# Winograd-Strassen products of an MLP: three products added from PSUM to two accumulators each, the square on ScalarE, all weight remainders on VectorE

## The reference

```python
for l in range(DEPTH):                                   # DEPTH = 2
    ...                                                  # two attention groups, output projection
    u = _rmsnorm(h, g_mlp[l])
    h = h + jnp.square(jax.nn.relu(u @ w_up[l])) @ w_down[l]   # 1024 -> 4096 -> 1024
return _rmsnorm(h, g_final)
```

## Time and profile before

| | us |
|---|---|
| executions | 1269.7, 1270.18, 1273.45 (median 1270.18) |
| profiled execution, its own time | 1274.95 |
| its span | 1273.1 |
| PE busy | 1221.1 (96%) |
| DVE busy | 954.5 (75%) |
| ACT busy | 567.3 (45%) |
| POOL busy | 646.1 (51%) |

### The profile page before, as it was taken

One profiled execution on the slowest core, in us unless ns is written; L12 is line 12 of the kernel. 1 busy time (PEld: TensorE's weight loads), 2 busy tenths in 40 slices (PEclk: granted clock), 3 DMA queues, 4 the chain that ended last, 5 costly groups with the idle time before them and its releaser, 6 DMA issues.

```text
span 1273.1 us, 16342 instructions
## 1 busy us (share of the span) xinstructions
PE 1221.1 (96%) x5812; PEld 1002.1 (79%) x5812; DVE 954.5 (75%) x1307; ACT 567.3 (45%) x906; POOL 646.1 (51%) x380
## 2 busy tenths in 40 slices
PE   8999899999899999999799998999989999999977
PEld 7887678888688888888688776888867888888866
DVE  5558867656878778779956687775687887877994
ACT  5245666743334333433333466675523343433323
POOL 1001234620997887876410023445059978788750
PEclk9899999999899999999899999999999999999989
DMA  6421101124134332340224220102423323432211
GB/s 185 113 69 59 42 17 34 50 83 133 52 114 132 100 99 84 116 132 27 73 62 109 58 66 9 34 27 90 133 67 117 100 81 100 133 100 94 72 33 67
DMA packets 128451, 104.04 MB, mean 82 GB/s; under 512 B 5442, under 2 KB 109940, under 8 KB 128372
## 3 DMA queue, kind: packets, MB, share of 16 engines
q1 hardware_dynamic: 128144, 102.97, 27.1%
q10 hardware_dynamic: 100, 0.03, 0.0%
q0 software_dynamic: 128, 0.00, 0.0%
HBM read 99.32 MB, written 2.10 MB: 80 GB/s over the span
## 4 chain that ended last, share of the span: by engine, by line
PE 84%; DVE 6%; issue 4%; ACT 2%; POOL 2%; DMA 2%; POOLq 0%; DVEq 0%; SPq 0%; ACTq 0%
PE bank L1421 73%; PE bank L1489 3%; PE bank L1517 2%; PE bank L1461 2%; DVE w_lo L1000 1%; PE bank L1446 1%; DMA stage<-in_w_up 1%; PE bank L1435 1%; DMA stage<-in_w_down 1%; ACT w_hi L721 1%; PE bank L1655 1%; DVE acc L1400 1%; DVE pt_lo L1062 0%; POOL raw L625 0%; DMA xin<-in_x 0%
## 5 line engine op out<-in xcount | busy, mean ns | idle before, releaser
L1421 PE MATMUL bank<-u_hi,w_hi 128*128 128x512 f32 x760 | 301.7, 397 | 9.7 <-DVE tmp_y L1359 8.1
L1421 PE MATMUL bank<-u_hi,w_lo 128*128 128x512 f32 x760 | 297.9, 392 | 0.0
L1421 PE MATMUL bank<-u_lo,w_hi 128*128 128x512 f32 x760 | 297.7, 392 | 0.0
L721 ACT ACTIVATE w_hi<-stage 128x1024 fp32r<-128x1024 f32 (+3 forms) x141 | 136.4, 976 | 221.1 <-PE bank L1421 92.8
L1000 DVE TENSOR_TENSOR w_lo<-stage,w_hi 128x1024 fp32r<-128x1024 f32 (+2 forms) x116 | 165.6, 1434 | 65.0 <-ACT w_hi L721 64.7
L1421 PEld LDWEIGHTS bank<-u_hi,w_hi 128*128 128x128 f32 x760 | 143.9, 189 | 42.6 <-issue 13.9
L1421 PEld LDWEIGHTS bank<-u_hi,w_lo 128*128 128x128 f32 x760 | 143.8, 189 | 30.7
L1421 PEld LDWEIGHTS bank<-u_lo,w_hi 128*128 128x128 f32 x760 | 144.0, 189 | 28.9
L721 ACT ACTIVATE w_hi<-b 128x1024 fp32r<-128x1024 f32 x84 | 88.5, 1059 | 164.2 <-PE bank L1421 101.2
L1421 PE MATMUL bank<-w_hi,quad_hi 128*128 128x512 f32 x392 | 152.7, 390 | 2.5 <-DVE sum L1340 2.5
L1421 PE MATMUL bank<-w_hi,quad_lo 128*128 128x512 f32 x392 | 152.5, 389 | 0.0
(11 more groups left out here) (225 smaller groups left out, 2498.9 us busy)
## 6 DMA issues: line engine op xcount, KB each, us to landing
stage<-in_w_up SPq DMA_DIRECT2D x64, 512.0 KB, 4.1
b<-in_w_down SPq DMA_DIRECT2D x56, 512.0 KB, 3.3
stage<-in_w_in SPq DMA_DIRECT2D x32, 512.0 KB, 3.9
stage<-in_w_out SPq DMA_DIRECT2D x16, 512.0 KB, 3.5
stage<-in_w_down SPq DMA_DIRECT2D x8, 512.0 KB, 3.4
xin<-in_x SPq DMA_DIRECT2D x4, 512.0 KB, 7.2
stage<-in_w_ukv SPq DMA_DIRECT2D x4, 512.0 KB, 3.3
out<-yout SPq DMA_DIRECT2D x4, 512.0 KB, 3.6
```

What stands on the lines that cost most here:

```text
L721: last = nc.scalar.activation(hi(w_hi, s)[:, :, d:d + n], st(r)[:, :, f:f + n], ACT.Copy)
L1421: mm = nc.tensor.matmul(acc, a, b, start=first and t == 0 and m == 0, stop=last and t == len(terms) - 1 and m == 2)
```

## The change

1. `low_by`: the remainders of the blocks of p4 to p6 are made by DVE, in the places where its list held none. POOL makes none for products.
2. No sum1, sum5, sum6. There is one more accumulator, `u2` (128 x 2 x 512), and the four corners of `acc`. p0 is added to the upper left corner and to u2, p3 to the lower right and upper right, p4 to the lower right and lower left; the others to one place. Each addition reads PSUM, so a chunk has 20 in place of 14. `evict` also waits for the product before it to be read.
3. u2 is added to three corners on POOL (128x1024 each), after p2, p3 and p4 of the last product chunk. DVE's p4 and p5 of that chunk wait for the first and second of these. The combinations of before are gone.
4. The activation: DVE makes max(psum,0)*rb in one instruction into one of two halves of `tmp_y`; ACT squares it (`square_up`), in its list behind the split of the same step. In chunk 7 ACT squares twice (rounded, and in place), and DVE's `hid_lo` waits for the second.
5. In chunk 1, DVE's `quad_lo` of chunk 0 stands behind the reading of the first projection instead of ahead of it.
6. The transpositions wait for all products read and for the first (or all three) additions of u2.

```diff
-    return "pool" if name in ("outd", "outm") or is_product(b) and i >= 4 or l > 0 and b < RING else "dve"
+    return "pool" if name in ("outd", "outm") or l > 0 and b < RING else "dve"
...
+        corner_of = [acc[:, 2 * r:2 * r + 2, d * SEQ:(d + 1) * SEQ] for r, d in ((0, 0), (0, 1), (1, 0), (1, 1))]
+        targets = [(corner_of[0], u2), (corner_of[0],), (u2,), (corner_of[3], corner_of[1]), (corner_of[3], corner_of[2]),
+                   (corner_of[1],), (corner_of[2],)]
...
-                for p in range(4, NP):
-                    out_low(l, at + p)
...
+                for k, p in ((2, 2), (1, 3), (3, 4)):
+                    pool.wait_ge(prod_read, val(prod_read, l, product_at(LAST - 1, p) + 2))
+                    corner = corner_of[k]
+                    nc.gpsimd.tensor_tensor(corner, corner, u2[:, :, :], ALU.add).then_inc(u2_added, 1)
...
+                def square_up(c, i):
+
+                    use = f"up{c}_{i}"
+                    y = tmp_y[:, i % 2, :]
+                    if c >= 2:
+                        act.wait_ge(qa_lo, val(qa_lo, l, 2 * (c - 1)))
+                        act.wait_ge(qs_lo, val(qs_lo, l, 4 * (c - 1)))
+                    act.wait_ge(*read_out(l, use))
+                    if c < LAST:
+                        nc.scalar.activation(raw[:, c % 2, i, :], y, ACT.Square).then_inc(hid_f, 1)
+                        return
+                    nc.scalar.activation(hid_hi[:, i, :], y, ACT.Square).then_inc(hid_hi_made, 1)
+                    act.wait_ge(hid_hi_made, val(hid_hi_made, l, i + 1))
+                    nc.scalar.activation(y, y, ACT.Square).then_inc(hid_f, 1)
...
+                    if n:
+                        dve.wait_ge(prod_read, val(prod_read, l, 2 * n + hf - 1))
+                    if c == LAST - 1 and p in (4, 5):
+                        dve.wait_ge(u2_added, val(u2_added, l, p - 3))
+                    for k, quad in enumerate(targets[p]):
+                        dst = quad[:, hf, :]
+                        if c == 0 and (p == 0 or p == 3 or p == 4 and k == 1):
+                            last = nc.vector.tensor_copy(dst, src)
+                        else:
+                            last = nc.vector.tensor_tensor(dst, dst, src, ALU.add)
+                    last.then_inc(prod_read, 1)
...
+                            nc.vector.scalar_tensor_tensor(out=tmp_y[:, i % 2, :], in0=bank[BANK[use]][:, :], scalar=0.0,
+                                                           in1=rb[:, :], op0=ALU.max, op1=ALU.mult
+                                                           ).then_inc(freed(use), 1)
+                            if c == 1 and i == 0:
+                                quads_low(0)
...
-                    pe.wait_ge(comb_left, val(comb_left, l, 4 if j < TT else 6))
+                    pe.wait_ge(prod_read, val(prod_read, l, product_at(LAST, 0)))
+                    pe.wait_ge(u2_added, val(u2_added, l, 1 if j < TT else 3))
```

78 lines of the change are left out of this document (20 added, 58 removed).

## The result

| | before | after |
|---|---|---|
| median of 4 executions, us | 1269.94 | 1241.12 |
| lowest and highest | 1268.67, 1273.45 | 1239.83, 1242.78 |
| profiled execution | 1274.95 | 1242.78 |
| its span | 1273.1 | 1241.0 |

The changed kernel takes 0.977 of the time before, 95% interval 0.9746 to 0.9793: 28.8 us less by the medians, 32.2 between the two profiled executions. The forecast was 10.7 less.

The account below looks back on a forecast made before the run. PE was taken to bound the kernel, without idle time in steady rounds, its idle time lying at the edges. The terms -15.0 - 4.7 + 5.0 + 4.0 = -10.7 took 1270.18 to 1259.5 us, range 1246 to 1281.

Parts of the forecast that it names:

- a gap of 3.01 us: PE at 944.68: the matmul behind it took 0.47, so the clock should stay at 2.4 GHz, 2.1 us per layer back.
- The loop: DVE's longest loop in a steady round: 37.9 us plus 2.5 standing behind POOL, 40.4 against PE's 40.8.
- rival 1: Steady rounds: POOL's blocking makes DVE's loop longer than PE's round, up to 2.1 us each, total +10.3, 1280.5; chance 0.22.
- layers' end, idle and clock: Last product stretch to first transposition: gains 4.8 and 6.0 us idle plus 2.1 clock per layer, 15.0 together, bounds 4 and 21.
- start of the MLPs: Waits of 4.66 and 3.01 go, POOL's chain to T2 and T4 is late next; gain 4.7 us, bounds 0 and 7.7.
- first rounds: First round of each layer: third projection's bank comes late, PE waits 2.5 us, twice 5.0, bounds 0 and 9.
- steady rounds: The 12 rounds run almost without a stall; 4.0 us charged in all, 0.33 each, bounds 0 and 25.
- I take 7.5 and add four readings, 9.9: Last product stretch: when DVE ends p0's reading, 9.9 us in, so last product read and first transposition at 27.4.
- The sign that was set for it: Steady round: DVE at its `quad_lo` 27 to 29 us in; 30 or more would mean PE waits before each third projection.
- The hedge: Steady rounds: DVE's six remainders may stand behind POOL's sums, 0 to 5 us in all; 2.5 was taken.
- rival 3: Whole kernel: everything fits, end gains 19, start 6, no stall, -25 us, 1245 to 1249; chance 0.12.
- Nothing on PE's path: cost nothing: Activation with the square on ACT: costs nothing and shortens DVE's part of a round by some 3 us.

Follow-up runs that it names:

- gap3: The changed kernel with 5 additional DVE instructions ahead of the last reading of a product in each layer's last product chunk; 1250.88 us.
- u_square_dve: The changed kernel with the activation's square moved from ACT back to DVE; 1267.88 us.
- u_low_pool: The changed kernel with the remainders of p4 to p6 moved from DVE back to POOL; 1240.41 us.

## Why the prediction came out wrong

**What held.** L1400 and L1404 went and PE's waits for them. PE's clock stayed at 2.4 GHz at both ends; the reason given, that a gap of 3.01 us had left it there, was not put to the test, for no gap remained, and gap3 shows that one of 2.49 can lower it. From E the last product was read 17.5 us later, as summed: 584.72 to 602.2. In the first round `quad_lo` was finished 32.2 us in (362.22 - 330.06) for 31.4 forecast (the working counts to its end), and p0's reading and POOL's chain to T2 were late next at the start, as said. The loop was 39.75 us where 40.4 was worked out, though that is partly luck: the working went by T2 and added 2.5 us for blocking, and the loop that the traces show goes by T4 and T1's remainder. The rounds of 41.43 in u_square_dve are rival 1's mechanism, had the square stayed; they cost 6.8 us there. The Trainium skill, "Perfetto Trace Analysis", section "Optimizing Scalar/DVE Operations", says that moving work between GpSimd and VectorE may not help. The runs agree: u_low_pool and the changed kernel take the same time, though not by the wait that rival 1 drew from it.

**What failed**, by the terms of the sum against the span:

| term | forecast | measured |
|---|---|---|
| layers' end, idle and clock | -15.0 | -7.7 - 8.8 - 3.2 - 2.6 = -22.3 |
| start of the MLPs | -4.7 | -8.7 (see 3) |
| first rounds | +5.0 | +0.8 + 0.6 = +1.4 |
| steady rounds | +4.0 | 0 |
| code ahead of the MLPs | 0 | -2.5 |
| sum | -10.7 | -32.1 |

1. *Steady rounds and E.* The working gave a loop of 40.4 us under a round of 40.8, and then charged for it all the same: 0.33 per round, and in "I take 7.5 and add four readings, 9.9" a DVE that comes to each last stretch late. A loop that is shorter than PE's round leaves nothing behind. DVE waits for PE in every round (2.85 us at 497.23), and E, here the end of p0's reading, becomes what PE and four readings make it: 12 x 0.227 + 4 x 0.60 = 5.1, measured 461.35 - 456.23 = 5.12 in the fourth stretch. The sign that was set for it, `quad_lo` 27 to 29 us into a steady round, came out at 24.5 (480.75 - 456.23). In the last stretch E is 6.1, one `hid_lo` later. With 6.1 the prediction's own step says 6.1 + 17.5 = 23.6, under the 24.49 at which PE is there: no gap at all, in place of 1 to 3 us. This one step is 4.0 of the steady rounds and 2 x 2.9 = 5.8 of the end, 9.8 of the 21.4 us between the two sums.

Timeline of DVE, a wait for PE in a steady round, then the last stretch from E to the reading of p6:

```profile
497.23 0.69 DVE L1375 SCALAR_TENSOR_TENSOR tmp_y<-bank,rb 128x512 f32<-128x512 f32 x1 [2.85 <-PE bank L1422]
...
584.72 1.21 DVE L1007 TENSOR_TENSOR w_lo<-b,w_hi 128x1024 fp32r<-128x1024 f32 x1
...
600.93 1.27 DVE L1361 TENSOR_TENSOR acc<-acc,bank 128x512 f32<-128x512 f32 x2
```

The hedge was for POOL's blocking, 2.5 us of it. It was taken into the sum, where it belonged into the range: by the sum itself rival 3 was the likeliest case.

2. *First rounds.* `quad_lo` was dated within 0.8 us, but PE's own lateness was left out: the 2.0 us that it waits in the first stretch move its demand for the bank too. Wait 0.80 and 0.62 in place of 2.5.

3. *Start.* The two pieces up to the last product stretch gave -7.3; less the +1.4 of point 2 that is -8.7 for the start. Of the waits, layer 0 gained 4.66 - 1.65 - 0.35 = 2.7 (forecast 2.8) and layer 1 3.01 + 0.45 + 2.51 - 0.33 - 1.64 - 0.31 = 3.7 (forecast 1.9; the 0.45 stands at 950.82 in the trace before). The other 2.3 are clock: the row that the prediction quoted, a matmul of 0.76 behind the wait of 4.66, is one at 1.2 GHz, and the 12 matmuls from there to 331.93 take 5.22 us where 12 at 2.4 GHz take 2.8. These 2.4 us were left out, though the same loss was counted at the layers' ends.

4. *Clock at the end.* Forecast 2.1 per layer, measured 3.2 and 2.6; the matmul and transposition rows themselves give 2.3 (4.17 to 2.76 and 1.97 to 1.04). The rest is put down to spread; no run separates it.

5. *The square's gain was sized too small.* "Nothing on PE's path: cost nothing" was right of its cost. As a gain the sum took 0.8 us of the loop and 1.19 and part of another of the start, and gave it no price of its own. It is the edit on which the rest hangs: 10.7 us alone, and 26.8 as the last of the four. It takes four instructions with two SBUF inputs per chunk off DVE, which were long because they stood behind POOL (1.19 on average, where one that does not stand takes 0.6 to 0.7), and which made POOL stand in turn. ACT squares a tile in 0.61 to 0.64.

The range ended at 1246 because rival 3 counted the end at 19 and the start at 6; they were 22 and 9.

## What to carry to other kernels

When a loop through two engines works out shorter than the bounding engine's round, charge nothing for it in the sum, and put the doubt into the range; then recompute where the helper engine stands at the edges, which is where the gain is. Room read ahead of one wait is not room in the round: a delay there can make two engines collide later on (2.8 us of work in a place with 3.6 us of room cost 1.7 per steady round). Before moving work between DVE and POOL, move what reads SBUF twice off both: here ACT had the room.
